# Expert rows returned to their tokens: token numbers through a table in device memory, a later request for half of the rows, and no padding matmuls in the last pair

## The chip, the cores and the metric

The kernel runs on one core of a Trainium2 chip. The metric is the device time of one execution in microseconds, lower is better; the number compared is the median over several runs. Everything is float32.

## What is computed

One layer of a hybrid backbone over 256 latent tokens of width 1024 (with 256 context tokens): a token mixer (neighbourhood attention, a gated scan and grouped-query attention, merged by gates), and then a mixture of experts. The change lies in the second part:

```python
def hierarchical_moe(h, w_gr, b_gr, w_er, b_er, w_gate, w_up, w_down):
    ...
    e_val, e_idx = lax.top_k(e_in, TOP_K)              # TOP_K = 2 of 16 experts
    w_sel = jax.nn.softmax(e_val, axis=-1) * p_group
    ...
    for e in range(N_EXPERTS):
        he = jax.nn.silu(h @ w_gate[e]) * (h @ w_up[e])
        y = y + combine[:, e:e + 1] * (he @ w_down[e])
    return y
```

After it the kernel adds `mod[5] * y` to the stream and applies a final RMS norm. Each token goes to a first and a second choice of expert.

## The kernel before

The expert part works on eight pairs of experts (pairs 0 to 7; LAST is 7). An expert has 64 slots for tokens (CAP), so a pair fills 128 slots. For each pair TensorE does, in this order: `gate` (16 matmuls with 512 columns, shown as 32 records, since every float32 matmul has two records), `up` (the same), the gathering of the first half of the next pair's tokens with a 0/1 selection matrix S (L1116), the turning of the hidden values (`turn_hidden`, L1186), the second half of that gathering, and `down` in two column halves (8 matmuls each, 16 records). `gate`, `up` and `down` are all recorded at L1163, in `two_experts`.

**Weights.** Each pair needs six halves of weights (gate 0, gate 1, up 0, up 1, down 0, down 1), numbered through as q = 0 to 47; a half is two loads of 1 MB, one for each expert (L387). They go through a ring of 11 places, and SyncE issues load after load on its queue, each as soon as its place is free. The last pair uses q = 42 to 47: up takes 44 and 45, down takes 46 and 47. TensorE waits for both loads of a half ahead of its first matmul (`take_half`).

**Rows of pairs 0 to 6.** VectorE scales a pair's result into `y_sb` (`experts_out`, L1722), and GpSimd writes its 128 rows with one indirect DMA (L565) to rows of the device array `y_rows`, which has one block of 256 rows for the first choices and one for the second. The row numbers stand in `token_rows`, one column for each pair. To make such a column, TensorE multiplies S with the token numbers (`tokens_of_slots`, L1126, 2 columns), and VectorE turns the sum into integers (`rows_of_tokens`, L1712). Rows out of bounds are skipped. Before `experts_out` writes `y_sb` again it waits for the write of the pair before.

**The return.** When the write of pair 6 has landed, GpSimd asks for `y_rows` in four reads of 512 KB (L570): two of first choices, two of second choices. VectorE multiplies each with the token's weight and adds it to `acc` (`gathered_back`, L1731).

**The last pair** stays on the chip: `scatter` multiplies the turned selection matrix with `y_sb` (L1210), one column half at a time, and VectorE adds the sums to `acc` (`scattered`, L1704). TensorE's order at the end is down 0, scatter 0, down 1, scatter 1. VectorE's order is: three reads gathered, `experts_out` of half 0, the fourth read gathered, `scattered` 0, `scaled_tokens` (L1697, the final gain on the first half of the columns), `experts_out` of half 1, `scattered` 1. After that only the final norm and the output are left.

**Padding.** In the last pair TensorE also runs matmuls whose result nobody reads (`stay_warm`, L1151): one ahead of each half of up, and two ahead of down 0.

All engines run their own instructions in order. Pairs over 64 tokens for an expert would go through later passes, which these inputs don't need.

Of the kernel before, what the change touches and what calls it, by code (L numbers as in the profile page):

```python
# [13 lines left out]
P = 128  # L14
D = 1024
KD = D // P
L = 256
# [124 lines left out]
def build(nc, d):  # L142

    ctx = ExitStack()
    with ctx:
# [121 lines left out]
        slot_of, slot_ok = keep(32, NT, NE), keep(4)  # L267
        slot_at, slot_w = keep(4), keep(4)
# [14 lines left out]
        token_of = keep(NT * NE, NT, NE)  # L283
# [42 lines left out]
        token_of_ready, token_sum, token_rows_ready = sem("token_of_ready"), sem("token_sum"), sem("token_rows_ready")  # L326
# [170 lines left out]
        def _(pool):  # L497
# [62 lines left out]

            pool.wait_ge(rows_cleared, 16 * 2 * NT)
            for n in range(LAST):
                pool.wait_ge(token_rows_ready, 2 * n + 2)
                pool.wait_ge(y_out, 2 * n + 2)
                pool.indirect_dma_start(d["y_rows"][:, :], bass.IndirectOffsetOnAxis(token_rows[:, n:n + 1], 0), y_sb, None,  # L565
                                        bounds_check=2 * L - 1, oob_is_err=False).then_inc(y_stored, 16)
            pool.wait_ge(up_ready, LAST)
            pool.wait_ge(y_stored, 16 * LAST)
            for q in range(2 * NT):
                pool.dma_start(y_back[:, q, :], d["y_rows"][q * P:q * P + P, :]).then_inc(y_in[q], 16)  # L570
# [177 lines left out]
        def _(pe):  # L748
# [371 lines left out]
            def tokens_of_slots(n, S):  # L1120

                pe.wait_ge(token_of_ready, 1)
                if n:
                    pe.wait_ge(token_rows_ready, 2 * n)
                for t in range(NT):
                    ins = pe.matmul(banks[7][:, 384 + 2 * n:386 + 2 * n], S[:, t, :], token_of[:, t, 2 * n:2 * n + 2],  # L1126
                                    start=(t == 0), stop=(t == NT - 1))
                ins.then_inc(token_sum, 1)

# [18 lines left out]
            def stay_warm(n):  # L1148

                for _ in range(n):  # L1150
                    pe.matmul(banks[1][:, :], ident, small[:, 0:512], start=True, stop=True)  # L1151

            def two_experts(bank, weights_at, parts, lhsT, q=None, n=None):

                for k in range(parts):
                    if q is not None and k % 4 == 0:
                        if q == 6 * LAST + 2:
                            stay_warm(1)
# [55 lines left out]
            for n in range(PAIRS):  # L1214
                gate(n, ring(6 * n), 6 * n)
                up(n, ring(6 * n + 2), 6 * n + 2)
                if n < LAST:
                    tokens_of_slots(n, S_now[n % 2])
                if n < LAST:
# [6 lines left out]
                for i in range(2):  # L1226
                    if n == LAST and i == 0:
                        stay_warm(2)
# [24 lines left out]
        def _(dve):  # L1253
# [11 lines left out]

            dve.memset(zeros, 0.0)
# [343 lines left out]
            def choices():  # L1610

                for j, oh in enumerate((oh1, oh2)):
                    link(dve.tensor_tensor(r_et, oh, slot_of, ALU.mult))
# [6 lines left out]
                dve.scalar_tensor_tensor(out=token_of, in0=oh2, scalar=float(L),  # L1620
                                         in1=sm("token").unsqueeze(2).broadcast_to([P, NT, NE]), op0=ALU.mult, op1=ALU.add)\
                   .then_inc(token_of_ready, 1)
# [84 lines left out]
            def rows_of_tokens(n):  # L1707

                dve.wait_ge(token_sum, n + 1)
                for e in range(2):  # L1710
                    part = slice(e * CAP, (e + 1) * CAP)
                    dve.tensor_scalar(token_rows[part, n:n + 1], banks[7][part, 384 + 2 * n + e:385 + 2 * n + e], 1024.0, None,  # L1712
                                      ALU.add).then_inc(token_rows_ready, 1)

# [24 lines left out]
            link(dve.tensor_tensor(slot_of, posm, sm("first_slot").unsqueeze(1).broadcast_to([P, NT, NE]), ALU.add))  # L1739
# [10 lines left out]
            for n in range(1, LAST + 1):  # L1750
# [3 lines left out]
                rows_of_tokens(n - 1)  # L1754
# [205 lines left out]
```

## Time and profile before

| | |
|---|---|
| median of 3 runs | 724.5 us (723.94 to 724.51) |
| the profiled execution's own time | 724.15 us |
| its span, first to last instruction | 722.4 us |
| busy: TensorE / VectorE / ScalarE / GpSimd | 701.3 / 296.9 / 112.2 / 172.6 us |
| expert pairs begin (first gathering) | 501.3 us |
| steady time of one pair | 25.4 us |
| last expert weights land, last row read lands | 702.2, 706.0 us |
| last matmul ends, last addition to `acc` ends | 715.7, 716.4 us |

Times of rows are microseconds from the first instruction. Matmuls are pipelined and their ends are modelled, so a row's end can stand up to some 0.1 us after the next row's start. What VectorE does is read best from its own timeline, and when a transfer was issued and landed from the views of its line.

### The profile page before, as it was taken

Reading aid. Unit: us, or ns where it says so; the run is one execution under the profiler, and the core shown is the slowest. Engines: PE = TensorE matmul, PEld = TensorE weight load, DVE = VectorE, ACT = ScalarE, POOL = GpSimd, SP = SyncE. Lnnn points to the kernel's source line nnn. Section 1 sums busy time; section 2 is a strip of 40 time slices with the busy share of each in tenths; the row PEclk is TensorE's granted clock in tenths of the full one; section 3 lists DMA queues with packets and bytes.
Section 4 is the critical chain, followed back from the end, with each engine's and each line's share of the span. In section 5 each row is a group of like instructions: output and inputs, shape, how many; then the busy total and the mean of one; then the engine's idle time right before and its main releaser. Section 6 shows DMA issues by size and latency. Waiting matters only on the chain.

```text
span 722.4 us, 7996 instructions
## 1 busy us (share of the span) xinstructions
PE 701.3 (97%) x3282; PEld 416.7 (58%) x3282; DVE 296.9 (41%) x507; ACT 112.2 (16%) x197; POOL 172.6 (24%) x126
## 2 busy tenths in 40 slices
PE   9999999999999999998999999999999999999995
PEld 5444586555775467776777788647434434443431
DVE  3439492778310475644343223325413212211315
ACT  4021011111000422221122230013000000000012
POOL 0008989789179000800000000000000000000010
PEclk9999999999999999999999999998999999999998
DMA  8994526762442332433481235995899999999991
GB/s 355 421 377 193 200 108 235 290 220 68 175 140 94 116 117 73 161 116 117 183 342 60 71 122 200 421 401 212 336 416 423 420 423 421 422 420 423 420 396 66
DMA packets 28933, 183.70 MB, mean 254 GB/s; under 512 B 3479, under 2 KB 5911, under 8 KB 13536
## 3 DMA queue, kind: packets, MB, share of 16 engines
q1 hardware_dynamic: 26880, 178.45, 62.4%
q0 software_dynamic: 1584, 3.97, 1.4%
q10 hardware_dynamic: 432, 0.75, 0.3%
q8 instruction: 27, 0.44, 0.2%
q14 instruction: 10, 0.08, 0.0%
HBM read 178.14 MB, written 6.82 MB: 256 GB/s over the span
## 4 chain that ended last, share of the span: by engine, by line
PE 91%; DMA 3%; DVE 2%; issue 2%; ACT 1%; SPq 0%; ACTq 0%; DVEq 0%; POOLq 0%
PE bank L1163 21%; PE bank L773 18%; PE bank L777 10%; PE bank L769 8%; PE bank L790 6%; PE bank L1116 4%; PE bank L995 4%; PE bank L796 4%; PE bank L920 2%; PE bank L941 2%; PE bank L822 2%; PE bank L928 2%; PE bank L783 2%; DMA y_rows<-sb,token_rows 1%; DMA sb<-y_rows 1%
## 5 line engine op out<-in xcount | busy, mean ns | idle before, releaser
L1163 PE MATMUL bank<-sb 128*64 128x512 f32 x768 | 167.5, 594 | 0.0
L773 PE MATMUL bank<-sb 128*128 128x256 f32 x576 | 128.5, 382 | 0.6 <-PE bank L769 0.3
L773 PEld LDWEIGHTS bank<-sb 128*128 128x128 f32 x576 | 108.1, 190 | 17.8 <-issue 3.8
L1163 PEld LDWEIGHTS bank<-sb 128*64 128x64 f32 x768 | 54.2, 137 | 106.7 <-issue 105.7
L565 POOL DMA_INDIRECT y_rows<-sb,token_rows x7 | 7.0, 997 | 371.5 <-DVE sb L1722 371.5
L525 POOL TENSOR_TENSOR sb<-sb 128x1024 f32<-128x1024 f32 x32 | 68.1, 2129 | 59.3 <-DMA sb<-ada_w 38.0
L1354 DVE COPY sb<-bank 128x512 f32<-128x512 f32 x45 | 29.2, 685 | 103.6 <-PE bank L928 66.2
L777 PE MATMUL bank<-sb 128*128 128x512 f32 x160 | 70.2, 593 | 0.3 <-PE bank L773 0.3
L769 PE MATMUL bank<-sb 128*128 128x512 f32 x128 | 55.8, 593 | 0.3 <-PE bank L995 0.3
L777 PEld LDWEIGHTS bank<-sb 128*128 128x128 f32 x160 | 29.9, 190 | 35.3 <-issue 35.3
L1687 DVE TENSOR_TENSOR sb<-sb,bank 128x512 f32<-128x512 f32 x8 | 5.5, 687 | 99.5 <-PE bank L1163 99.5
L790 PE MATMUL bank<-sb 128*128 128x256 f32 x192 | 42.2, 380 | 0.6 <-PE bank L790 0.6
L769 PEld LDWEIGHTS bank<-sb 128*128 128x128 f32 x128 | 23.9, 190 | 29.3 <-issue 29.3
L790 PEld LDWEIGHTS bank<-sb 128*128 128x128 f32 x192 | 36.2, 190 | 6.3 <-issue 1.5
L529 POOL TENSOR_TENSOR sb<-sb 128x512 f32<-128x512 f32 x24 | 35.7, 1488 | 1.9
L1116 PE MATMUL bank<-sb 128*128 128x128 f32 x256 | 31.7, 278 | 0.3 <-issue 0.3
L530 POOL TENSOR_TENSOR sb<-sb 128x512 f32<-128x512 f32 x24 | 30.6, 1273 | 1.9
L1116 PEld LDWEIGHTS bank<-sb 128*128 128x128 f32 x256 | 29.8, 192 | 0.4 <-issue 0.4
L995 PE MATMUL bank<-sb 128*128 128x512 f32 x64 | 29.0, 599 | 0.7 <-DVE sb L1306 0.7
L1678 DVE TENSOR_SCALAR sb<-bank,sb 128x128 f32<-128x128 f32 x64 | 21.9, 405 | 19.0 <-PE bank L1116 19.0
L661 ACT ACTIVATE sb<-bank,sb 128x512 f32<-128x512 f32 x32 | 21.8, 685 | 40.9 <-DVE sb L1469 40.8
L796 PE MATMUL bank<-sb 128*128 128x512 f32 x64 | 27.8, 592 | 0.0
(246 smaller groups left out, 684.2 us busy)
## 6 DMA issues: line engine op xcount, KB each, us to landing
sb<-expert_w SPq DMA_DIRECT2D x94, 1024.0 KB, 19.3
sb<-front_w SPq DMA_DIRECT2D x19, 2048.0 KB, 8.1
sb<-ada_w SPq DMA_DIRECT2D x32, 512.0 KB, 3.5
sb<-ada_mix SPq DMA_DIRECT2D x4, 2048.0 KB, 20.4
sb<-xcT SPq DMA_DIRECT2D x4, 512.0 KB, 6.2
sb<-front_w SPq DMA_DIRECT2D x4, 512.0 KB, 21.1
y_rows<-sb SPq DMA_DIRECT2D x4, 512.0 KB, 23.2
sb<-expert_w SPq DMA_DIRECT2D x4, 512.0 KB, 5.6
```

The costliest lines, as they stand in the source:

```text
L525: link(pool.tensor_tensor(w, w, cvec[:, k0:k0 + PART_K, 0:1].broadcast_to([P, PART_K, 512]), ALU.mult))
L529: link(pool.tensor_tensor(w[:, 0, :], w[:, 0, :], w[:, 1, :], ALU.add))
L530: ins = pool.tensor_tensor(ada_sum[g], ada_sum[g], w[:, 0, :], ALU.add)
L769: ins = pe.matmul(ps[:, :], lhs(w, k, i * P), hT[:, k, :], start=(k == 0), stop=(k == KD - 1))
L773: ins = pe.matmul(ps[:, c * L:(c + 1) * L], lhs(w, k, (2 * i + c) * P), hT[:, k, 0:L], start=(k == 0), stop=(k == KD - 1))
L777: ins = pe.matmul(ps[:, :], hT[:, k, i * P:(i + 1) * P], w[:, k * 512:(k + 1) * 512], start=(k == 0), stop=(k == KD - 1))
L790: ins = pe.matmul(ps[:, c * L:(c + 1) * L], lhs(w, k, (2 * i + c) * P, D), src[:, k, :], start=(k == 0), stop=(k == 3))
L796: ins = pe.matmul(ps[:, :], yT[:, k, i * P:(i + 1) * P], w[:, k * 512:(k + 1) * 512], start=(k == 0), stop=(k == KD - 1))
L995: ins = pe.matmul(banks[BANK_OF[i]][:, :], lhs(slot[0], k, i * P), hT[:, k, :], start=(k == 0), stop=(k == KD - 1))
L1116: ins = pe.matmul(banks[i][:, c * P:(c + 1) * P], x_nat[:, t, (4 * i + c) * P:(4 * i + c + 1) * P], S[:, t, :], start=(t == 0), stop=(t == ...
L1163: ins = pe.matmul(bank[e * CAP:(e + 1) * CAP, :], lhsT[:, k, e * CAP:(e + 1) * CAP], weights_at(k, e), start=(k == 0), stop=(k == parts - 1))
L1354: dve.tensor_copy(dst, shared_wait(n)[:, :]).then_inc(shared_out, 1)
```

## The change

- GpSimd gets a table in device memory, `slot_tokens`, with one number for each slot of pairs 0 to 6 (896 integers). It is first filled with 1024 (out of bounds) from a VectorE memset, at a quiet time. When the choices are known, VectorE works out for every token and choice its row in the table (`table_rows`) and the number to write there (`token_ids`). GpSimd writes them with four indirect DMAs of 128 numbers, waits for them, and reads the table back into `token_rows` with one DMA. After that all seven columns of row numbers are there.
- `tokens_of_slots` (TensorE) and `rows_of_tokens` (VectorE) go, for all seven pairs. `token_of` goes, two small VectorE instructions for `token_ids` and two for `table_rows` come.
- The two reads of second choices are issued only after weight half q = 46 (down 0 of the last pair) has landed. The two of first choices are issued as before.
- All `stay_warm` matmuls go.
- VectorE's order at the end becomes: `experts_out` half 0, four reads gathered, `scattered` 0, `experts_out` half 1, `scaled_tokens`, `scattered` 1.

```diff
+            table = d["slot_tokens"].rearrange("(p n) o -> p (n o)", n=LAST)
+            pool.wait_ge(rows_unused, 1)
+            pool.dma_start(table, token_rows[:, :]).then_inc(table_cleared, 16)
+            pool.wait_ge(ids_ready, 2)
+            pool.wait_ge(table_rows_ready, 1)
+            pool.wait_ge(table_cleared, 16)
+            for q in range(2 * NT):
+                pool.indirect_dma_start(d["slot_tokens"][:, :], bass.IndirectOffsetOnAxis(table_rows[:, q:q + 1], 0),
+                                        token_ids[:, q:q + 1], None, bounds_check=STORED - 1, oob_is_err=False)\
+                    .then_inc(table_filled, 16)
+            pool.wait_ge(table_filled, 16 * 2 * NT)
+            pool.dma_start(token_rows[:, :], table).then_inc(token_rows_in, 16)
+            pool.wait_ge(token_rows_in, 16)
             pool.wait_ge(rows_cleared, 16 * 2 * NT)
             for n in range(LAST):
-                pool.wait_ge(token_rows_ready, 2 * n + 2)
                 pool.wait_ge(y_out, 2 * n + 2)
                 pool.indirect_dma_start(d["y_rows"][:, :], bass.IndirectOffsetOnAxis(token_rows[:, n:n + 1], 0), y_sb, None,
                                         bounds_check=2 * L - 1, oob_is_err=False).then_inc(y_stored, 16)
             pool.wait_ge(up_ready, LAST)
             pool.wait_ge(y_stored, 16 * LAST)
             for q in range(2 * NT):
+                if q == NT:
+                    pool.wait_ge(w_in_[RING[(HALVES - 2) % len(RING)]], landed(HALVES - 2))
                 pool.dma_start(y_back[:, q, :], d["y_rows"][q * P:q * P + P, :]).then_inc(y_in[q], 16)
...
-            def tokens_of_slots(n, S):
-
-                pe.wait_ge(token_of_ready, 1)
-                if n:
-                    pe.wait_ge(token_rows_ready, 2 * n)
-                for t in range(NT):
-                    ins = pe.matmul(banks[7][:, 384 + 2 * n:386 + 2 * n], S[:, t, :], token_of[:, t, 2 * n:2 * n + 2],
-                                    start=(t == 0), stop=(t == NT - 1))
-                ins.then_inc(token_sum, 1)
...
-            def stay_warm(n):
-
-                for _ in range(n):
-                    pe.matmul(banks[1][:, :], ident, small[:, 0:512], start=True, stop=True)
...
                     if q is not None and k % 4 == 0:
-                        if q == 6 * LAST + 2:
-                            stay_warm(1)
                         take_half(q + k // 4)
...
                 if n < LAST:
-                    tokens_of_slots(n, S_now[n % 2])
-                if n < LAST:
                     gather(n + 1, S_now[(n + 1) % 2], (0,))
...
                 for i in range(2):
-                    if n == LAST and i == 0:
-                        stay_warm(2)
                     down(n, i, ring(6 * n + 4 + i), 6 * n + 4 + i)
...
+            dve.memset(token_rows[:, :], 1024).then_inc(rows_unused, 1)
             dve.memset(zeros, 0.0)
...
-                dve.scalar_tensor_tensor(out=token_of, in0=oh2, scalar=float(L),
-                                         in1=sm("token").unsqueeze(2).broadcast_to([P, NT, NE]), op0=ALU.mult, op1=ALU.add)\
-                   .then_inc(token_of_ready, 1)
+                link(dve.scalar_tensor_tensor(out=table_at, in0=slot_ok, scalar=-4096.0, in1=slot_at, op0=ALU.mult, op1=ALU.add))
+                dve.tensor_scalar(table_rows[:, :], table_at, 4096.0, None, ALU.add).then_inc(table_rows_ready, 1)
+                for j in range(2):
+                    dve.tensor_scalar(token_ids[:, NT * j:NT * j + NT], sm("token"), float(L * j), None, ALU.add)\
+                       .then_inc(ids_ready, 1)
...
                 modulate(n)
-                rows_of_tokens(n - 1)
...
             gated(LAST)
             turned_out(LAST)
-            gathered_back(range(2 * NT - 1))
             experts_out(LAST, (0,))
-            gathered_back((2 * NT - 1,))
+            gathered_back(range(2 * NT))
             scattered(LAST, (0,))
+            experts_out(LAST, (1,))
             dve.wait_ge(glast_in, 16)
             dve.wait_ge(scat_out, NT)
             scaled_tokens()
-            experts_out(LAST, (1,))
             scattered(LAST, (1,))
```

## Rows read from the trace of the kernel before

**Rows 1.** The page: the chain that ended last, by engine.
```profile
PE 91%; DMA 3%; DVE 2%; issue 2%; ACT 1%; SPq 0%; ACTq 0%; DVEq 0%; POOLq 0%
```
**Rows 2.** Busy time by stretch: length, PE, PEld, DVE, ACT, POOL, granted clock, DMA share, GB/s.
```profile
660.00:680.00 20.00, 20.00 (x114) 9.57 (x112) 4.07 (x12) 1.19 (x2) 0.21 (x1) 1.00 1.02 422
...
703.00:704.00 1.00, 1.00 (x8) 0.30 (x6) 1.00 (x2) 0.19 (x1) 0.00 (x0) 1.00 0.59 242
```
**Rows 3.** The chain in pair 6 (start, us, what), line L1126 alone, VectorE's timeline in pair 6.
```profile
671.41 0.54 PE bank L1126 x4
...
L1126 PE MATMUL bank<-sb x28: 251/251/272, 518.9 to 671.7; 128*128 128x2 f32 x28
...
671.51 0.69 DVE L1687 TENSOR_TENSOR sb<-sb,bank 128x512 f32<-128x512 f32 x1 [13.10 <-PE bank L1163]
```
**Rows 4.** TensorE's timeline in the last pair: start, us, instructions, idle time before.
```profile
689.88 1.13 PE L1151 MATMUL bank<-sb 128*128 128x512 f32 x2
...
694.52 1.13 PE L1151 MATMUL bank<-sb 128*128 128x512 f32 x2
695.58 3.65 PE L1163 MATMUL bank<-sb 128*64 128x512 f32 x16
...
702.38 3.65 PE L1163 MATMUL bank<-sb 128*64 128x512 f32 x16
707.22 1.96 PE L1210 MATMUL bank<-sb 128*128 128x512 f32 x4 [1.18 <-DVE sb L1722]
...
713.71 1.95 PE L1210 MATMUL bank<-sb 128*128 128x512 f32 x4 [0.95 <-DVE sb L1722]
```
**Rows 5.** Single weight loads of L387: issue time and, below, us from issue to landing.
```profile
L387 SPq DMA_DIRECT2D sb<-expert_w x1: 2122/2122/2122, 663.0 to 663.0; - x1
DMA to landing us min/median/max: 28.2/28.2/28.2
L387 SPq DMA_DIRECT2D sb<-expert_w x1: 6286/6286/6286, 665.6 to 665.6; - x1
DMA to landing us min/median/max: 30.5/30.5/30.5
```
**Rows 6.** The chain's step over the last row write, and the four reads' landings.
```profile
684.65 9.46 DMA y_rows<-sb,token_rows
...
L570 POOL DMA_DIRECT2D sb<-y_rows x4: 550/558/569, 694.7 to 696.3; - x4
...
DMA to landing us min/median/max: 7.7/8.7/9.7
```
**Rows 7.** VectorE's timeline at the end.
```profile
706.38 0.69 DVE L1722 TENSOR_TENSOR sb<-bank,sb 128x512 f32<-128x512 f32 x1
707.16 1.28 DVE L1731 SCALAR_TENSOR_TENSOR sb<-sb 128x1024 f32<-128x1024 f32 x1
708.52 1.38 DVE L1704 TENSOR_TENSOR sb<-sb,bank 128x512 f32<-128x512 f32 x2
710.00 1.29 DVE L1697 TENSOR_TENSOR sb<-sb 128x512 f32<-128x512 f32 x2
712.87 0.69 DVE L1722 TENSOR_TENSOR sb<-bank,sb 128x512 f32<-128x512 f32 x1 [1.58 <-PE bank L1163]
...
715.70 0.69 DVE L1704 TENSOR_TENSOR sb<-sb,bank 128x512 f32<-128x512 f32 x1 [0.17 <-PE bank L1210]
```
**Rows 8.** ScalarE's timeline: the copy of the last pair's turned hidden values.
```profile
700.77 0.60 ACT L708 ACTIVATE sb<-bank 128x512 f32<-128x512 f32 x1 [10.18 <-PE bank L1186]
```
**Rows 9.** TensorE's timeline and, below, busy time by stretch (columns as above) around 492 us.
```profile
491.37 3.79 PE L1078 MATMUL bank<-sb 128*128 128x20 f32 x24
...
493.00:495.00 2.00, 2.00 (x12) 2.00 (x11) 0.00 (x0) 0.51 (x1) 0.00 (x0) 0.50 1.04 438
```
**Rows 10.** GpSimd's first row write and the VectorE instruction that waits for it (timelines).
```profile
532.36 1.18 POOL L565 DMA_INDIRECT y_rows<-sb,token_rows  x1 [225.15 <-DVE sb L1722]
...
552.73 0.69 DVE L1722 TENSOR_TENSOR sb<-bank,sb 128x512 f32<-128x512 f32 x1 [1.59 <-PE bank L1163]
```

More of the change, by code:

```diff
@@ L266, in build @@
         passes_f = keep(1)
-        slot_of, slot_ok = keep(32, NT, NE), keep(4)
-        slot_at, slot_w = keep(4), keep(4)
+        table_of, slot_ok = keep(32, NT, NE), keep(4)
+        slot_at, slot_w, table_at = keep(4), keep(4), keep(4)
         SW_now, ST_now = at(C0 + 6144, NT, P), at(C0 + 6144 + NT * P, NT, P)
@@ L282, in build @@
         token_rows = ctx.enter_context(nc.sbuf_tensor("token_rows", [P, LAST], I32))
-        token_of = keep(NT * NE, NT, NE)
+        token_ids = ctx.enter_context(nc.sbuf_tensor("token_ids", [P, 2 * NT], I32))
+        table_rows = ctx.enter_context(nc.sbuf_tensor("table_rows", [P, 2 * NT], I32))
         masks = ctx.enter_context(nc.sbuf_tensor("masks", [P, LEVELS - 1, P], I8))
@@ L325, in build @@
         choice_ready = sem("choice_ready")
-        token_of_ready, token_sum, token_rows_ready = sem("token_of_ready"), sem("token_sum"), sem("token_rows_ready")
+        rows_unused, ids_ready, table_rows_ready = sem("rows_unused"), sem("ids_ready"), sem("table_rows_ready")
+        table_cleared, table_filled, token_rows_in = sem("table_cleared"), sem("table_filled"), sem("token_rows_in")
         rows_cleared = sem("rows_cleared")
@@ L1612, in choices @@
                 for j, oh in enumerate((oh1, oh2)):
-                    link(dve.tensor_tensor(r_et, oh, slot_of, ALU.mult))
+                    link(dve.tensor_tensor(r_et, oh, table_of, ALU.mult))
                     link(dve.tensor_reduce(slot_at[:, NT * j:NT * j + NT], r_et, AX.X, ALU.add))
@@ L1705, in scattered @@
                         ins.then_inc(scat_out, 1)
[L1707 to L1713, printed above, removed]
             def experts_out(n, halves=range(2)):
@@ L1738, in _ @@
             count_passes()
-            link(dve.tensor_tensor(slot_of, posm, sm("first_slot").unsqueeze(1).broadcast_to([P, NT, NE]), ALU.add))
+            link(dve.scalar_tensor_tensor(out=table_of, in0=posm, scalar=float(LAST),
+                                          in1=sm("first_row").unsqueeze(1).broadcast_to([P, NT, NE]), op0=ALU.mult, op1=ALU.add))
             choices()
@@ L1808 @@
                       ("ones", P), ("upto", P), ("iota", CAP), ("limits", MAXPASS - 1),
-                      ("rank", NE), ("first_slot", NE), ("token", NT), ("g_ffn", KD), ("lb", 8), ("hg_g", 1),
+                      ("rank", NE), ("first_row", NE), ("token", NT), ("g_ffn", KD), ("lb", 8), ("hg_g", 1),
                       ("gqn", HD), ("gqn_swapped", HD), ("gkn", HD), ("gkn_swapped", HD),
@@ L1826, in shape_constants @@
     rank = np.arange(NE, 0, -1, dtype=f)
+    e = np.arange(NE)
+    first_row = np.where(e < 2 * LAST, e % 2 * CAP * LAST + e // 2 - LAST, 4096).astype(f)
     t = np.arange(L)
@@ L1839, in shape_constants @@
         "limits": np.tile(np.arange(1, MAXPASS, dtype=f) * CAP, (P, 1)),
-        "rank": np.tile(rank, (P, 1)), "first_slot": np.tile(np.arange(NE, dtype=f) * CAP - 1, (P, 1)), "token": (i[:, None] + P * np.arange(NT)[None, :] - 1024).astype(f), "cos": cos.astype(f), "sin": sin.astype(f),
+        "rank": np.tile(rank, (P, 1)), "first_row": np.tile(first_row, (P, 1)), "token": (i[:, None] + P * np.arange(NT)[None, :]).astype(f), "cos": cos.astype(f), "sin": sin.astype(f),
     }
@@ L1956 @@
     d["y_rows"] = nc.dram_tensor("y_rows", (2 * L, D), F32).ap()
+    d["slot_tokens"] = nc.dram_tensor("slot_tokens", (STORED, 1), I32).ap()
     build(nc, d)
```

## The prediction

> **What bounds the kernel now.** I read the chain of work that ended last first: TensorE holds 91% of it [rows 1], so what leaves TensorE's queue counts unless something else is late behind it. The second view is the busy time by stretch: from 520 us on TensorE is busy all the time and so are the 16 DMA engines, at 422 GB/s [rows 2]. Both are full, so the question is which one has slack. For that I set the landing of single weight loads against the timeline of TensorE. Counted back from the last load, the second load of half 45 is issued at 663.0 and lands at 691.2, and that of half 46 is issued at 665.6 and lands at 696.1 [rows 5]; TensorE uses them at 695.6 and 702.4 [rows 4]. So TensorE is the bound, but the weights are only 4.4 and 6.3 us ahead of it, and an earlier release of places doesn't hasten them, since the engines are full. The last view is the end on VectorE. The four reads of rows are issued from 694.7 to 696.3 and land 7.7 to 9.7 us later, the last at 706.0 [rows 6]. The chain runs through the write of pair 6 and these reads to `gathered_back` and then to `experts_out` of half 0 at 706.38, just behind down 0, which ends at 706.03 [rows 4, 7]. Two paths are thus nearly tied there: both must get shorter, or nothing is gained.
>
> **Token numbers off TensorE.** L1126 has 28 records, four to a pair, and four take 0.54 us of the chain [rows 3]: 7 x 0.54 = 3.8 us, all ahead of gate of pair 7. The two VectorE instructions that go with each lie beside matmuls: nothing. The turning of the hidden values comes 0.54 us sooner behind up, but in pair 6 VectorE has `he` ready at 672.2 (671.51 + 0.69), and up ended at 671.4 with 1.9 us of gathering to come [rows 3], so it is still there.
>
> **The table.** It hangs on GpSimd, which waits for nothing else then. The choices are ready at about 510.5 us. Four indirect DMAs cost up to 1.2 us each by the row of the first row write, and 0.7 us between them: 518. Their landing and that of the read back aren't in this trace. From above I take the 9.5 us of the last row write, twice, from below 2.2 us, twice, the page's shortest landing (the pieces of the output). The column is then there between 523 and 538 us; the first row write is now at 532.4 [rows 10]. At worst it slips by 6 us. Behind it on GpSimd are only the other row writes, and the one who waits for it is `experts_out` of pair 1 at 552.7 [rows 10]: a write issued at 538 that takes 9 us has landed at 547. Cost zero; the cover ends when the write is issued later than about 543.5, and TensorE feels it only later still, when VectorE is late for pair 2's `he` at about 570. The clearing of the table and the extra memset lie in times in which their engines wait, and three more VectorE instructions of 0.2 us fall into its 7 us of idle time ahead of 519 us: zero.
>
> **Padding off TensorE.** One matmul ahead of each half of up moves the next by 1.06 us (694.52 to 695.58, and the same ahead of the first half), two ahead of down 0 end at 702.38 [rows 4]. But the copy of the turned hidden values ends at 701.4 [rows 8], so down 0 couldn't start before 701.5: there only 0.9 us is gained, and a gap takes the place of the rest. With the weights there in time the shift at down 0 would be 3.8 + 2.1 + 0.9 = 6.8 us.
>
> **What is late next: weight half 45.** Half 44 would be wanted at 689.9 - 3.8 = 686.1. Its second load lands two loads before the second one of half 45, and a load is 2.5 us at 422 GB/s, so at about 686: just in time. Half 45 would be wanted at 686.1 + 3.6 = 689.7 and lands at 691.2, so TensorE waits 1.5 us. Up ends at 691.2 + 3.6 = 694.8 instead of 699.2, down 0 starts 2.3 us later, as now from the end of up to the end of the copy, at 697.1 (half 46 landed at 696.1), and ends at 700.7. The shift is 5.3 us, not 6.8. `experts_out` of half 0 is done at 701.5 (0.1 + 0.69), scatter 0 runs from 701.65 to 703.55, and down 1 ends at 707.15; its half 47 had landed at 702.2, and the DMA share falls only in the slice from 703 us [rows 2].
>
> **The reads.** The write of pair 6 lands 3.8 us sooner, at 690.3 instead of 694.1 [rows 6]. The two reads of first choices are issued at 690.9 and 691.5 and land at about 698.6 and 699.8, ahead of `experts_out` of half 0. Those of second choices wait for half 46. They are the last instructions of GpSimd, so nothing is queued behind this wait, and VectorE alone waits for them. Landed at 696.1, with the 0.55 us from landing to issue that shows now, they are issued at 696.65 and 697.2. With 7.7 and 8.3 us [rows 6] they land at 704.4 and 705.5. The four 512 KB reads share the engines with the last weights; the first two now meet half 46, and may hold it up by some tenths: I take 705.7 for the last. For the duration the bounds are 5.6 us (the page's median for 512 KB pieces of weights) and 9.7 us. The order of requests moves, the bytes don't: the engines still have to carry the last weights and 2.1 MB of rows. The Trainium skill ("DMA: Bandwidth & Descriptors", section on the anatomy of a DMA on the gpsimd path) gives such a DMA about 2.0 us and its bytes at 436 GB/s, 3.2 us for 512 KB. This trace has 7.7 to 9.7 us with four reads and the weights in flight, and speaks against it. By the rule the last read would land by 701 us, and VectorE would be bound by its own work: 0.4 us less in the sum.
>
> **VectorE's end.** From 701.5 it gathers two reads (1.29 each) to 704.1, the third on landing to 705.7, the fourth from 705.7 to 707.0. `scattered` 0 takes 1.38 to 708.45, `experts_out` of half 1 is done at 709.15 (down 1 had ended at 707.15), scatter 1 starts at 709.3 and its first token block is there at 710.4. `scaled_tokens` (1.29) now lies beside it and ends at 710.5. Two additions of 0.69 with what lies between them end at 712.15. Now the last one ends at 716.39 [rows 7]. What follows is unchanged. **Sum: 716.39 - 712.15 = 4.2 us.** The profiled execution took 724.15 us, so 719.9; the median of the runs stands 0.35 us above it: **720.2 us**.
>
> **Rival 1, no waiting for weights.** If half 45 lands with its present lead over what TensorE needs (for instance because the row write of pair 6 now falls elsewhere in its way), `experts_out` of half 0 is done at 699.9, VectorE never waits for a read, and its own chain ends at 710.2 or so: 6.1 us gained, 718.4. Against it: the row write moves to an earlier time, into the stretch that carries halves 44 and 45.
>
> **Rival 2, the second choices come late.** The first reads hold up half 46 by the time of their 1 MB (2.5 us), and the second reads take 9.7 us: the last lands at 709, VectorE ends at 715.4 at worst, 714.5 more likely: 722.5. For it: of the last load now the landing is 702.2 where its neighbours are about 2.5 us apart and it is 4.0 us behind, so reads do slow weights.
>
> **Rival 3, the clock: the other side.** The trace shows the granted clock at 0.50, 1.2 GHz, from 493 us, while TensorE was never idle but ran 20-column matmuls [rows 9], and it stays low for some 6.8 us, to 499.7. The change takes the padding out of such a place: between up and down 0 of the last pair there would be 2.3 us with six records of short transposes and gaps, where now the two padding matmuls fill 1.8 us. The Trainium skill ("TensorE: Matmul & The Clock Gate", part 1) says that the throttled clock is the default and activity releases it; by that rule the padding has a use and this part of the change is wrong. The rows show that light work can cost the clock, but also that the gaps of 1.18 and 0.95 us near the end don't [rows 4]: the granted clock stays at 1.00 up to 715 us. Price: the work from down 0 on is 3.6 + 1.95 + 3.6 + 1.95 = 11.1 us at 2.4 GHz [rows 4]. A fall at 697 us for 6.8 us adds 3.4 us to down 0, VectorE then gathers all four reads behind it, and the end comes at about 715.2: 723.3, still faster. If the clock stays low to the end, all of it doubles, and the last addition ends at about 721.9: 729.9 us, slower. It decides from about 5.7 us added: more than half of those 11.1 us at 1.2 GHz.
>
> **Rival 4, the table is late.** If its small DMAs took not 2 to 9.5 us each but over 30 us in all, pair 1's `experts_out` would wait, and beyond 25 us more TensorE too: 725 us or above. Nothing in the rows speaks for it. That rows land in wrong places would be no matter of time.
>
> **How the numbers follow.** Chances: the forecast 0.60 (719.2 to 721.8), rival 1 0.12, rival 2 0.14, rival 3 0.10 (half of it with the short fall), rival 4 and the unforeseen 0.04. The bounds of the reads give 719.8 to 721.6, a half 46 delayed by 2.5 us 723.5, rival 1 718.4; the range is 718.0 to 723.8. 0.2% is 1.45 us, about what a measurement of this kernel can tell from no change. Faster by more than that (below 723.05) are the forecast, rival 1 and most of rival 2: 0.85. Within it are the rest of rival 2 and the short fall: 0.08. Slower are the long fall and rival 4: 0.07.
>
> **What the profile after would show.** L1126, L1712 and L1151 are gone and a pair takes 24.9 us instead of 25.4; if not, something waits there. In the last pair a gap of about 1.5 us stands ahead of the second half of up, released by a weight load (rival 1: no gap), and one of about 0.9 us ahead of down 0. The first row write is at 538 us or before, and `experts_out` of pair 1 doesn't wait for it. The write of pair 6 is issued at 680.9; the last read lands at 705.7. `experts_out` of half 1 starts behind `scattered` 0, not behind down 1: VectorE, held by the reads, is the bound at the end. The granted clock is 1.00 up to the last matmul. The prediction is wrong if the clock falls before it, if the reads of second choices land beyond 709, or if TensorE waits for weights already in pair 6, where I reckon with a lead of over 5 us.

## The result: slower, with the weights late and TensorE waiting

| | before | changed |
|---|---|---|
| median | 724.5 us (6 runs, 723.94 to 725.38) | 728.06 us (6 runs, 726.35 to 728.74) |
| ratio to before | | 1.0042 (95% interval 1.003 to 1.0054) |
| profiled execution, its span | 724.15, 722.4 us | 726.35, 723.9 us |
| down 0 of the last pair starts | 702.4 us | 703.6 us |
| last addition to `acc` ends | 716.4 us | 717.95 us |

The prediction said 720.2 us, 718.0 to 723.8, with 0.85 for faster. It was wrong in sign. The profiled execution is the fastest of the six, so the profile shows the least of the loss; the ratio counts all of them.

The steady part is as predicted: L1126, L1712 and L1151 of before are gone and a pair takes 24.96 us. But in the last pair TensorE's timeline shows what [rows 4] doesn't, four waits for weights (columns as there; `two_experts` is L1162 now, scatter L1209):

```profile
673.36 10.79 PE L1162 MATMUL bank<-sb 128*64 128x512 f32 x48
685.43 3.66 PE L1162 MATMUL bank<-sb 128*64 128x512 f32 x16 [1.27 <-DMA sb<-expert_w]
691.10 5.35 PE L1162 MATMUL bank<-sb 128*64 128x512 f32 x16 [2.01 <-DMA sb<-expert_w]
696.80 3.65 PE L1162 MATMUL bank<-sb 128*64 128x512 f32 x16 [0.35 <-DMA sb<-expert_w]
...
703.60 3.65 PE L1162 MATMUL bank<-sb 128*64 128x512 f32 x16 [1.64 <-DMA sb<-expert_w]
708.20 1.96 PE L1209 MATMUL bank<-sb 128*128 128x512 f32 x4 [0.94 <-DVE sb L1712]
710.09 3.65 PE L1162 MATMUL bank<-sb 128*64 128x512 f32 x16
715.27 1.96 PE L1209 MATMUL bank<-sb 128*128 128x512 f32 x4 [1.53 <-DVE sb L1712]
```

Down of pair 6 still starts 2.6 us sooner than before (673.36 instead of 676.0). Then the second half of gate waits for half 43, the two halves of up wait for 44 and 45, and by 696.80 TensorE is 1.2 us behind before. The first half of up takes 5.35 us for what takes 3.65. That is no second wait for weights: TensorE is busy all the time, and the granted clock is 0.50, so it runs at 1.2 GHz there, behind the idle gap of 2.01 us (columns as in [rows 2]):

```profile
691.50:694.50 3.00, 3.00 (x10) 1.15 (x8) 0.00 (x0) 0.00 (x0) 0.05 (x1) 0.50 1.00 415
```

This cost nothing at the end, because half 45 landed only at 696.7: at full clock TensorE would have waited longer for it. The last wait for weights is for half 46: down 0 could have begun at about 702.6, behind the copy of the turned values, and begins at 703.60. The chain that ended last says the same; it has one load of half 46 in it where before it had the row write and the reads [rows 6]:

```profile
670.39 33.07 DMA sb<-expert_w
703.47 0.14 issue
703.60 3.67 PE bank L1162 x16
```

The single load, issue and landing time as in [rows 5]: half 46 lands 33.1 us after 670.4, at 703.5. Before it was 696.1. Half 45 (667.7 + 29.0) lands at 696.7 instead of 691.2.

```profile
L389 SPq DMA_DIRECT2D sb<-expert_w x1: 6280/6280/6280, 670.4 to 670.4; - x1
DMA to landing us min/median/max: 33.1/33.1/33.1
```

The engines weren't idle. The place where the stream fell behind is found by going through the busy time by stretch of both kernels from left to right. First the changed kernel, then before, both columns as in [rows 2]; the last number is GB/s:

```profile
512.00:516.00 4.00, 4.00 (x20) 1.29 (x18) 0.75 (x2) 0.60 (x1) 3.09 (x4) 1.00 1.04 383
516.00:520.00 4.00, 4.00 (x23) 1.66 (x20) 0.51 (x1) 0.00 (x0) 0.37 (x1) 1.00 1.02 271
520.00:524.00 4.00, 4.00 (x36) 3.60 (x36) 2.03 (x7) 0.60 (x1) 0.00 (x0) 1.00 0.96 182
510.00:530.00 20.00, 20.00 (x112) 9.26 (x110) 6.98 (x23) 1.19 (x2) 4.56 (x5) 1.00 1.00 313
```

```profile
516.00:520.00 4.00, 4.00 (x23) 1.82 (x20) 0.69 (x1) 0.00 (x0) 0.00 (x0) 1.00 1.01 426
520.00:524.00 4.00, 4.00 (x35) 3.62 (x35) 1.71 (x6) 0.60 (x1) 0.00 (x0) 1.00 1.01 426
510.00:530.00 20.00, 20.00 (x112) 9.47 (x110) 6.76 (x21) 1.19 (x2) 0.00 (x0) 1.00 1.01 412
```

The DMA share is the same 1.0, but from 510 to 530 us the engines move 313 instead of 412 GB/s: 20 us x 99 GB/s = 2.0 MB less, which is 4.8 us of the stream. The busy share alone hides it. At that time GpSimd writes the table, four indirect DMAs of 128 four-byte numbers each, at most 2 KB in all (a number whose row is out of bounds, as for tokens of the last pair, is skipped):

```profile
511.48 1.04 POOL L570 DMA_INDIRECT slot_tokens<-token_ids,table_rows  x1 [203.28 <-DVE token_ids L1619]
...
524.83 0.58 POOL L574 DMA_DIRECT2D token_rows<-slot_tokens  x1 [8.46 <-DMA slot_tokens<-token_ids,table_rows]
532.09 0.99 POOL L579 DMA_INDIRECT y_rows<-sb,token_rows  x1 [6.68 <-DVE sb L1712]
```

GpSimd itself isn't late: the first row write is at 532.09 (532.36 in [rows 10]) and waits for VectorE, not for the table.

At the end VectorE is no longer held by the reads. It does all four in one go behind down 0 (compare [rows 7]):

```profile
707.36 0.69 DVE L1712 TENSOR_TENSOR sb<-bank,sb 128x512 f32<-128x512 f32 x1 [5.78 <-PE bank L1162]
707.97 5.19 DVE L1721 SCALAR_TENSOR_TENSOR sb<-sb 128x1024 f32<-128x1024 f32 x4
```

**Theory T** from here on: the table's small writes hold up the weight stream by 4.8 us, and the rest of the change is sound. **Rival R**: the table is harmless, and the earlier reads, the gate and the new order at the end are at fault.

### The profile page after: what moved, and what is told of

Same layout as the page of the kernel before. It is cut to its first block, busy times and chain, and to the rows that moved or that the text cites. A ratio compares the mean times of both kernels' runs of the same rounds, so it can differ in the third digit from the quotient of the medians.

```text
span 723.9 us, 7913 instructions
## 1 busy us (share of the span) xinstructions
PE 697.2 (96%) x3246; PEld 413.1 (57%) x3246; DVE 292.8 (40%) x497; ACT 112.2 (15%) x197; POOL 177.4 (25%) x132
## 4 chain that ended last, share of the span: by engine, by line
PE 80%; SPq 9%; DMA 6%; DVE 3%; issue 1%; ACT 1%; ACTq 0%; DVEq 0%
PE bank L789 18%; PE bank L1162 12%; PE bank L793 10%; SPq L389 9%; PE bank L785 8%; PE bank L806 6%; DMA sb<-expert_w 5%; PE bank L1011 4%; PE bank L812 4%; PE bank L1132 3%; PE bank L936 2%; PE bank L957 2%; PE bank L838 2%; PE bank L944 2%; PE bank L799 2%
## 5 line engine op out<-in xcount | busy, mean ns | idle before, releaser
L1162 PE MATMUL bank<-sb 128*64 128x512 f32 x768 | 169.8, 599 | 5.3 <-DMA sb<-expert_w 5.3
L1162 PEld LDWEIGHTS bank<-sb 128*64 128x64 f32 x768 | 55.0, 138 | 113.3 <-issue 106.2
L527 POOL TENSOR_TENSOR sb<-sb 128x1024 f32<-128x1024 f32 x32 | 66.6, 2081 | 59.9 <-DMA sb<-ada_w 36.0
L793 PE MATMUL bank<-sb 128*128 128x512 f32 x160 | 70.2, 593 | 0.3 <-PE bank L789 0.3
L785 PE MATMUL bank<-sb 128*128 128x512 f32 x128 | 55.8, 593 | 0.3 <-PE bank L1011 0.3
L570 POOL DMA_INDIRECT slot_tokens<-token_ids,table_rows x4 | 4.0, 994 | 204.2 <-DVE token_ids L1619 203.3
L1132 PE MATMUL bank<-sb 128*128 128x128 f32 x256 | 31.8, 278 | 0.3 <-issue 0.3
L1011 PE MATMUL bank<-sb 128*128 128x512 f32 x64 | 29.0, 599 | 0.7 <-DVE sb L1302 0.7
```

Of the source, the lines that this page charges most:

```text
L527: link(pool.tensor_tensor(w, w, cvec[:, k0:k0 + PART_K, 0:1].broadcast_to([P, PART_K, 512]), ALU.mult))
L785: ins = pe.matmul(ps[:, :], lhs(w, k, i * P), hT[:, k, :], start=(k == 0), stop=(k == KD - 1))
L793: ins = pe.matmul(ps[:, :], hT[:, k, i * P:(i + 1) * P], w[:, k * 512:(k + 1) * 512], start=(k == 0), stop=(k == KD - 1))
L1011: ins = pe.matmul(banks[BANK_OF[i]][:, :], lhs(slot[0], k, i * P), hT[:, k, :], start=(k == 0), stop=(k == KD - 1))
L1132: ins = pe.matmul(banks[i][:, c * P:(c + 1) * P], x_nat[:, t, (4 * i + c) * P:(4 * i + c + 1) * P], S[:, t, :], start=(t == 0), stop=(t == ...
L1162: ins = pe.matmul(bank[e * CAP:(e + 1) * CAP, :], lhsT[:, k, e * CAP:(e + 1) * CAP], weights_at(k, e), start=(k == 0), stop=(k == parts - 1))
```

## Experiments

The kernels were measured in four sessions, with the kernel before measured again beside them in each; the last column is its median there. These medians differ by 1.4 us, and its executions in the later three sessions spread from 723.4 to 730.3 us. Kernels of different sessions are therefore better compared by their ratios than by their medians.

| kernel | median us | ratio (95%) | before us |
|---|---|---|---|
| changed | 728.06 | 1.0042 (1.003 to 1.0054) | 724.5 |
| tail_only | 721.34 | 0.9937 (0.9916 to 0.9957) | 725.47 |
| table_only | 727.5 | 1.003 (1.0012 to 1.0047) | 725.47 |
| table_twice | 732.5 | 1.0081 (1.0048 to 1.0114) | 725.47 |
| dead4 | 726.72 | 0.9996 (0.9971 to 1.0022) | 725.86 |
| dead512 | 722.88 | 0.9958 (0.9938 to 0.9977) | 725.86 |
| dead4_spread | 721.77 | 0.9941 (0.9921 to 0.9961) | 725.86 |
| table_spread | 721.57 | 0.9954 (0.9931 to 0.9976) | 724.88 |
| tail_old_order | 727.24 | 1.0017 (0.9993 to 1.0042) | 724.88 |
| tail_ungated | 721.38 | 0.994 (0.992 to 0.996) | 724.88 |
| gather | 726.2 | 1.0018 (0.9999 to 1.0037) | 725.47 |
| gather_used | 720.58 | 0.9934 (0.9909 to 0.9959) | 725.86 |
| gather_used_pad | 719.92 | 0.9912 (0.988 to 0.9943) | 724.88 |

### The two halves of the change, apart

**tail_only** is the kernel before with the three edits that don't concern the table (padding, gate on the second choices, VectorE's order):

```diff
-                        if q == 6 * LAST + 2:
-                            stay_warm(1)
...
-                    if n == LAST and i == 0:
-                        stay_warm(2)
...
+                if q == NT:
+                    pool.wait_ge(w_in_[RING[(HALVES - 2) % len(RING)]], landed(HALVES - 2))
...
-            gathered_back(range(2 * NT - 1))
             experts_out(LAST, (0,))
-            gathered_back((2 * NT - 1,))
+            gathered_back(range(2 * NT))
             scattered(LAST, (0,))
+            experts_out(LAST, (1,))
...
             scaled_tokens()
-            experts_out(LAST, (1,))
```

> Tail parts alone: the kernel before without padding matmuls, with the new VectorE order and the gated second reads, token numbers still by TensorE. Theory T (the table's 4-byte writes hold up the weight stream by about 4.8 us): the weights land as before, so up ends at 697.1, down 0 at 703.0, the last addition at about 714.0: 2.4 us faster than before, about 722. Rival R (the new requests and order at the end are at fault, the table is harmless): at least 2 us slower than before, 727.

**table_only** is the changed kernel with those three edits taken back.

> Table alone: token numbers through the table, but padding, VectorE order and ungated reads as before. Theory T: the weight stream is 2 MB (4.8 us) behind from 530 us on, TensorE waits in the last pair in spite of being 3.8 us earlier: slower than before, 727 to 729. Rival R: TensorE saves 3.8 us and the reads come as much earlier: 720.7.

Measured: 721.34 and 727.5 us. R is dead: the end of the change alone gains 0.6%, and the table alone loses 0.3% in spite of the matmuls it takes from TensorE. The two don't add up: together they lose 0.42%. While down 0 waits for half 46, a shorter way to it is worth nothing. In tail_only no wait for weights shows in the last pair; down 0 starts at 698.99 behind the copy:

```profile
675.98 20.83 PE L1158 MATMUL bank<-sb 128*64 128x512 f32 x96
...
698.99 3.65 PE L1158 MATMUL bank<-sb 128*64 128x512 f32 x16 [0.69 <-ACT sb L710]
```

### Is it the small writes, and what about them?

**table_twice** is the changed kernel with the four writes repeated into a spare array ahead of the read back:

```diff
+            for q in range(2 * NT):
+                pool.indirect_dma_start(d["spare_table"][:, :], bass.IndirectOffsetOnAxis(table_rows[:, q:q + 1], 0),
+                                        token_ids[:, q:q + 1], None, bounds_check=STORED - 1, oob_is_err=False)\
+                    .then_inc(table_filled, 16)
```

> The changed kernel with its four small writes issued a second time, into a spare array. Theory T: the stream loses its 2 MB a second time and every later half lands 4.8 us later: 732 to 733, 4 to 5 us above the changed kernel. Rival R: four more small DMAs beside the matmuls cost nothing at the end: 728.

Measured: 732.5 us, 4.4 us above the changed kernel by the medians, about as T had it (7.0 above before in its session, where the changed kernel was 3.6 above before in its own: 3.5 by that). From 510 to 540 us the busy time by stretch has 284 GB/s (before: 411): 3.8 MB lost, nearly twice the 2.0, and half 46 lands at 708.6 (675.6 + 33.0), 5.1 us later than in the changed kernel. In the traced execution, 6.3 us above the changed kernel's, down 0 also ran at granted clock 0.50 and took 5.32 us for 3.65, so 1.7 us of that are the clock's.

**dead4** adds the writes to tail_only with nobody reading them, and the two VectorE instructions that make their row numbers; TensorE's work stays as in tail_only:

```diff
+            for q in range(2 * NT):
+                pool.indirect_dma_start(d["dead"][:, :], bass.IndirectOffsetOnAxis(table_rows[:, q:q + 1], 0),
+                                        ident[:, q:q + 1], None, bounds_check=STORED - 1, oob_is_err=False)\
+                    .then_inc(table_filled, 16)
+            pool.wait_ge(table_filled, 16 * 2 * NT)
```

> tail_only (721.3 us) plus four indirect writes of 128 numbers of 4 bytes, to the rows of the table, which nobody reads; token numbers still by TensorE. Theory T (these writes alone hold the stream up, whoever uses them): about 2 MB fewer weights between 510 and 530 us, halves 42 to 47 land 4.8 us later, 726 to 728. Rival (the read back, or TensorE's earlier pace, is what made weights late): 721 to 722.

**dead512** writes `ident[:, :]`, 512 bytes a piece, and **dead4_spread** writes 4 bytes again, but to row numbers times 128.

> As dead4, but each of the 128 pieces of a write has 512 bytes instead of 4 (256 KB in all). If the small size of a piece is the cause: only the bytes cost, 0.6 us of the stream, and 721 to 722. If the number of pieces or of indirect DMAs is the cause: as dead4, 726 to 728.

> As dead4, 4-byte pieces again, but each 512 bytes or more from the next in device memory. If pieces that share a block of memory wait for each other: much less than dead4, 721 to 723. If a 4-byte piece is slow by itself: as dead4, 726 to 728.

Measured: 726.72, 722.88 and 721.77 us, against 721.34 without any of them. Three stretches of dead4, and the same three of dead4_spread:

```profile
516.00:520.00 4.00, 4.00 (x25) 1.76 (x21) 0.69 (x1) 0.00 (x0) 0.29 (x1) 1.00 1.36 406
520.00:524.00 4.00, 4.00 (x36) 3.73 (x36) 1.60 (x5) 0.60 (x1) 0.00 (x0) 1.00 0.71 64
510.00:530.00 20.00, 20.00 (x114) 9.50 (x112) 7.11 (x23) 1.20 (x2) 4.13 (x4) 1.00 1.01 330
```

```profile
516.00:520.00 4.00, 4.00 (x25) 2.04 (x22) 0.69 (x1) 0.00 (x0) 0.00 (x0) 1.00 1.02 422
520.00:524.00 4.00, 4.00 (x35) 3.55 (x35) 1.93 (x6) 0.60 (x1) 0.00 (x0) 1.00 1.02 430
510.00:530.00 20.00, 20.00 (x114) 9.61 (x112) 6.82 (x21) 1.20 (x2) 4.12 (x4) 1.00 1.01 409
```

So at most 512 writes of 4 bytes into an array of 3.5 KB bring 422 to 430 GB/s down to 64 for 4 us. The share of 1.36 in one slice and 0.71 in the next says that single slices are rough here; over the 20 us it is 330 instead of 412 GB/s in tail_only, 1.6 MB. The same number of the same writes cost nothing that can be seen when their targets lie 512 bytes or more apart. The number of pieces, their size alone and the indirect form are each ruled out, and so is the read back, which dead4 doesn't have. That writes into one block of device memory wait for each other is the likeliest reason; the runs show the dependence on the distance, not the mechanism. How far apart is enough was not tried.

dead512 lies 1.5 us above tail_only, where 0.6 was expected for its bytes. Its trace puts this ahead of the writes. The gathering for pair 0 (L1128 there, L1118 in tail_only) runs at granted clock 0.50 and takes 6.45 instead of 3.81 us, so gate of pair 0 begins 2.0 us later (506.96 instead of 505.00), and the first of the writes is issued only at 513.09. First dead512, with its busy time by stretch, then tail_only:

```profile
500.57 6.45 PE L1128 MATMUL bank<-sb 128*128 128x128 f32 x32
501.00:506.00 5.00, 5.00 (x25) 5.00 (x25) 1.94 (x8) 0.00 (x0) 0.00 (x0) 0.50 0.00 0
```

```profile
501.26 3.81 PE L1118 MATMUL bank<-sb 128*128 128x128 f32 x32 [0.35 <-issue]
505.00 5.37 PE L1158 MATMUL bank<-sb 128*64 128x512 f32 x24
```

It helps to count from the start of that gate to the end of the last addition to `acc`: 208.35 us in tail_only, 208.35 in dead512, 208.36 in dead4_spread and 210.78 in dead4. In the traced executions only the dense writes cost anything.

The executions vary: dead4 ran from 723.08 to 728.87 us, dead4_spread from 721.44 to 723.19. The four of dead4 up to 724.16 have a mean granted clock of 0.995 to 0.997, the six from 726.68 on one of 0.990 to 0.994. The traced one (724.09) is of the first kind, so how much of the median's 5.4 us above tail_only is the stream and how much the clock is not shown. In the traced one it is 2.4 us, and TensorE waits for weights for 3.0 us there.

**table_spread** is the test on the change itself, with only the distance changed:

```diff
-            table = d["slot_tokens"].rearrange("(p n) o -> p (n o)", n=LAST)
+            table = d["slot_tokens"].rearrange("(p n w) o -> p n (w o)", n=LAST, w=P)[:, :, 0:1]
...
-                dve.tensor_scalar(table_rows[:, :], table_at, 4096.0, None, ALU.add).then_inc(table_rows_ready, 1)
+                dve.tensor_scalar(table_rows[:, :], table_at, 4096.0, float(P), ALU.add, ALU.mult).then_inc(table_rows_ready, 1)
```

> The changed kernel whole, only its table's numbers stand 512 bytes apart (row number times 128). Theory S (4-byte writes close together in device memory hold up the stream; the rest of the change is sound): the stream is on time, the last addition ends at about 712, 719.5 to 721, clearly faster than before. Rival: the read back, now 896 pieces of 4 bytes, holds the stream up in its turn: 723 or above.

Measured: 721.57 us, faster than before by 0.46%. The median lies 0.6 us above the expected end, its runs spread from 720.44 to 725.38, and 13 GB/s are still missing over the 20 us against before (0.26 MB, 0.6 us), with 368 GB/s in the slice in which the table is read back in 896 pieces:

```profile
524.00:528.00 4.00, 4.00 (x20) 1.29 (x18) 1.73 (x5) 0.00 (x0) 0.00 (x0) 1.00 1.02 368
...
510.00:530.00 20.00, 20.00 (x112) 9.22 (x110) 6.84 (x22) 1.19 (x2) 5.00 (x5) 1.00 1.01 399
```

The changed kernel's last addition ends 5.0 us later than this one's (717.95 and 712.97), where the difference in lost bytes is worth 4.2 us. By the ratios the two kernels lie 6.4 us apart; what the rest is stays open.

The run also splits the delay of the last halves. Its half 46 is issued at 666.2 and lands 31.8 us later, at 698.0:

```profile
L389 SPq DMA_DIRECT2D sb<-expert_w x1: 6303/6303/6303, 666.2 to 666.2; - x1
DMA to landing us min/median/max: 31.8/31.8/31.8
```

696.1 before, 698.0 here, 703.5 in the changed kernel: 5.5 us come with the dense table. Of the other 1.9 us, 0.6 are the missing 0.26 MB. The row write and the first reads are asked for some 3 and 4.5 us sooner than before, but they don't show as the reason for the rest: gather_used, below, asks for them as early (680.91 and 690.37) and has half 46 at 695.5. It carries some 0.2 MB less in its software queue than before; what the difference is stays open.

### The parts of the end

**tail_old_order** is tail_only with VectorE's old order, **tail_ungated** is tail_only with all reads asked for at once.

> tail_only (721.3 us) with VectorE's old order at the end (three reads gathered ahead of experts_out of half 0), padding still gone, reads still gated. If the two paths are tied as the prediction said: down 0 is done sooner, but experts_out of half 0 comes only after the reads, at about 706: 724 to 725, no gain over before. Rival (dropping the padding is the whole gain, the order doesn't matter): 721 to 722.

> tail_only (721.3 us) with all four reads asked for at once, as before. There the wait for half 46 held the reads of second choices back for only 0.4 us, so: 721 to 722, no difference. Rival (the gate protects the last weights, down 0 or down 1 waits without it): 723 or above.

Measured: 727.24 and 721.38 us. The gate is worth nothing here (its wait was 0.4 us). Without the new order the end gains nothing, and I had expected less of a loss: without padding and in the old order the kernel isn't at 724 to 725 but at 727.24. TensorE's timeline and the stretches with the granted clock show why:

```profile
699.22 3.65 PE L1158 MATMUL bank<-sb 128*64 128x512 f32 x16 [0.69 <-ACT sb L710]
707.80 3.75 PE L1205 MATMUL bank<-sb 128*128 128x512 f32 x4 [4.92 <-DVE sb L1715]
711.48 3.79 PE L1158 MATMUL bank<-sb 128*64 128x512 f32 x16
```

```profile
704.00:708.00 4.00, 0.20 (x1) 0.23 (x2) 3.69 (x5) 0.00 (x0) 0.00 (x0) 0.62 0.14 56
708.00:710.00 2.00, 2.00 (x3) 0.94 (x4) 1.15 (x2) 0.00 (x0) 0.00 (x0) 0.50 0.00 0
```

Down 0 is done sooner, but `experts_out` still stands behind three reads, TensorE is idle for 4.92 us, the granted clock falls to 0.50 (1.2 GHz), and scatter 0 takes 3.75 instead of 1.95 us. This is the clock of the prediction's rival 3, though at another place, which the changed order closes. It agrees with the Trainium skill ("TensorE: Matmul & The Clock Gate", part 1), by which the throttled clock is the default and activity releases it. The new order with the padding kept was not run, so what the order is worth by itself isn't known.

### A way without token numbers

**gather** drops the table and the matmuls alike: `y_sb` is stored in slot order, and the reads pick the rows by token.

```diff
-                pool.indirect_dma_start(d["y_rows"][:, :], bass.IndirectOffsetOnAxis(token_rows[:, n:n + 1], 0), y_sb, None,
-                                        bounds_check=2 * L - 1, oob_is_err=False).then_inc(y_stored, 16)
+                pool.dma_start(d["y_rows"][n * P:n * P + P, :], y_sb).then_inc(y_stored, 16)
...
-                pool.dma_start(y_back[:, q, :], d["y_rows"][q * P:q * P + P, :]).then_inc(y_in[q], 16)
+                pool.indirect_dma_start(y_back[:, q, :], None, d["y_rows"][:, :], bass.IndirectOffsetOnAxis(row_of[:, q:q + 1], 0),
+                                        bounds_check=STORED - 1, oob_is_err=False).then_inc(y_in[q], 16)
```

> No table and no token numbers at all: y_sb is stored in slot order by plain DMAs, and the four returned reads become indirect reads with one row number for each token and choice (nothing is cleared first). No padding, new VectorE order, reads not gated. Theory T: nothing stalls the stream, TensorE is 3.8 us earlier: about 720, as the prediction's sum had it. Rival R (early reads hold up the last weights): 724 or above.

Measured: 726.2 us, a miss. I had overlooked that a plain store carries empty slots too, where the indirect one skips them. Its software queue, and that of the next kernel:

```profile
q0 software_dynamic: 1584, 5.54, 1.9%
```

```profile
q0 software_dynamic: 1584, 3.75, 1.3%
```

TensorE waits 2.59 us for weights ahead of 689.93, before the first read is issued at 690.34, so that wait isn't the reads' doing. It waits again ahead of down 0, and there the clock falls as well (TensorE's timeline and a stretch):

```profile
702.12 5.08 PE L1139 MATMUL bank<-sb 128*64 128x512 f32 x16 [2.17 <-DMA sb<-expert_w]
702.00:705.00 3.00, 2.88 (x8) 1.14 (x10) 0.00 (x0) 0.40 (x2) 0.00 (x0) 0.50 1.02 419
```

Down 0 takes 5.08 instead of 3.65 us: 1.4 us of the miss are the clock, at the very place where rival 3 had it.

**gather_used** stores only used slots, with row numbers from the experts' counts (six small VectorE instructions beside gate of pair 0), and gates the second choices:

```diff
-                pool.dma_start(d["y_rows"][n * P:n * P + P, :], y_sb).then_inc(y_stored, 16)
+                pool.indirect_dma_start(d["y_rows"][:, :], bass.IndirectOffsetOnAxis(store_rows[:, n:n + 1], 0), y_sb, None,
+                                        bounds_check=STORED - 1, oob_is_err=False).then_inc(y_stored, 16)
```

> No table, no token numbers; rows are stored at their slot's place, but only the used slots (row numbers from the experts' counts, empty ones out of bounds), so the stores carry 1.8 MB as before and not the 3.7 MB of the run gather; the returned reads are indirect, those of second choices wait for half 46; no padding, new VectorE order. Theory T plus: what made gather slow was its 1.9 MB more of stores, 4.4 us of the stream; here they are gone: 719 to 720, at or below tail_only. Rival (indirect reads are slow in themselves): 724 or above.

Measured: 720.58 us. The 1.8 MB are gone and with them 5.6 us by the medians (the bytes are worth 4.3 us; the two kernels also differ in gather's half clock in down 0, in the gate, worth nothing in tail_ungated, and in the early clearing). But its last scatter ran at half clock, behind an idle gap of 2.23 us:

```profile
708.53 3.09 PE L1199 MATMUL bank<-sb 128*128 128x512 f32 x4 [2.23 <-DVE sb L1710]
```

```profile
708.50:712.00 3.50, 3.09 (x4) 0.82 (x4) 2.11 (x4) 1.36 (x5) 0.00 (x0) 0.60 0.02 5
```

**gather_used_pad** fills that gap:

```diff
                     if n == LAST:
+                        if i == 1:
+                            for _ in range(2):
+                                pe.matmul(banks[3][:, :], ident, small[:, 0:512], start=True, stop=True)
                         scatter(n, (i,))
```

> gather_used (720.6 us; the granted clock fell to 0.50 after an idle gap of 2.2 us ahead of the last scatter, which then took 3.1 instead of 1.95 us) with two matmuls whose result nobody reads between down 1 and scatter 1. If that clock loss is real and the gap its place: last scatter at full clock, 1 us less, 719.5. Rival (the fall comes by chance, or elsewhere): 720.5, and the padding may cost up to 0.3 us.

```profile
708.24 1.98 PE L1218 MATMUL bank<-sb 128*128 128x512 f32 x4
710.89 1.96 PE L1199 MATMUL bank<-sb 128*128 128x512 f32 x4 [0.67 <-DVE sb L1713]
```

Measured: 719.92 us, the lowest median of all, 0.9% below before. The scatter is back at 1.96 us. The gain over gather_used is 0.7 of the expected 1 us, and the two intervals overlap, so that the padding pays is shown by the trace and not by the times. The traced execution is the slowest of its six: its gathering for pair 0 took 6.61 us at granted clock 0.50, as in dead512. From the start of pair 0's gate to the last addition it needs 206.84 us, gather_used 207.88.

## Why the prediction was wrong, point by point

- **The table, "cost zero": this is the step that failed.** I priced its DMAs as latency of GpSimd and asked who waits for their landing. That part held: the column was there at 530.7 (524.83 + 5.9), inside my 523 to 538. What I didn't price is what they do to the engines they share with a stream that I had just found full and only 4.4 us ahead of TensorE. The price was 2.0 MB, 4.8 us of the stream. Rival 4 had the right culprit at 0.04, but as a wait of `experts_out` in pair 1, which never came.
- **The landing times of [rows 5], taken as fixed: wrong.** I took them so because the engines are full ("the bytes don't" move). They hold only while nothing lowers what full engines carry.
- **Token numbers off TensorE: right as a mechanism, 3.8 us was too much.** A pair takes 24.96 instead of 25.40 us, so 0.44 and not 0.54 us are saved for each, 3.1 in all. It is lost again at halves 43 to 46.
- **Half 45 as the next limit: right as a mechanism.** In table_spread TensorE waits 1.39 us there, where the sum had 1.5; in gather_used 0.61.
- **Half 46 "held up by some tenths": open.** In table_spread it lands 1.9 us later than before, near the 2.5 us of rival 2, and TensorE is idle for 1.19 us ahead of down 0 instead of the 0.69 us that the copy takes in tail_only. But in gather_used, with the reads as early, it lands at 695.5, not later than before.
- **Padding and order, 0.9 us at down 0 and the rest: right.** In tail_only the last addition ends at 713.35 against 714.0 expected. In table_spread it ends at 712.97 and in gather_used at 712.34, where the prediction's sum had 712.15. Its sum was thus near that of a kernel whose table costs nothing. That it comes so near gather_used is partly luck: 1.1 us of the 712.34 are the scatter at half clock, which the sum doesn't have.
- **Rival 3, the clock: not the cause of the loss, but the fall came.** I had written that the clock would stay at 1.00 up to the last matmul. In the changed kernel it was 0.50 from 691.5 to 694.5 us, in up, where the wait for half 45 hid the loss; from 701 to 720 us it is 1.00 in every slice. In gather and table_twice it fell at the place that rival 3 named, ahead of down 0, and cost 1.4 and 1.7 us. Each time TensorE had first waited for weights.
- **The gate on second choices**: in the changed kernel it released the reads at 703.95, 7 us later than in the sum, because half 46 was late; even so VectorE didn't wait for them, since all moved together.
- **The chances don't add up to what is said of them.** By their parts "slower" is 0.05 + 0.04 = 0.09 and not 0.07. That changes nothing in the verdict.

## What to carry to other kernels

When the engines are full and a stream is only just ahead of its user, every DMA has two prices: its latency for whoever waits, and what it takes from the stream; the second is read from GB/s by stretch, not from the busy share, which stayed at 1.0 while a quarter of the bandwidth was gone. Scatter small numbers to targets well apart in device memory, or find a form that needs no numbers (reading by index what was stored in order), and let empty rows be skipped. Padding matmuls and the order of work on the engine that TensorE waits for belong together: dropped without the new order the padding left 727.2 us, with it 721.3. Late weights open gaps as well, and in three of the traced kernels without padding the clock fell behind one; in table_only, which has the padding and waits for the same weights, it stayed at 1.00.

## What the hardware showed that I had not expected

- At most 512 four-byte writes into 3.5 KB of device memory take 1.6 to 2.0 MB from a stream of about 420 GB/s; in the worst 4 us of dead4 it ran at 64 GB/s. The same writes at 512 bytes or more apart: 422 to 430 GB/s. The Trainium skill ("DMA: Bandwidth & Descriptors", specifications) says that below 512 bytes an engine reads, modifies and writes. That covers both forms alike, and only the dense one was slow here: for pieces of 4 bytes it is the distance that decides in these runs.
- Executions of one kernel differ by more than the change is worth: 6 us between the fastest and the slowest run of dead4, with the lower mean clock in the slower ones.
- The granted clock fell to 0.50 behind idle gaps of 4.92 us (tail_old_order), 2.23 (gather_used), 2.17 (gather), 2.01 (the changed kernel) and 1.81 us (table_twice). It stayed at 1.00 behind gaps of 2.59 us (gather) and 2.01 and 1.88 us (table_twice), and behind those of 0.9 to 1.5 us near the end. So the length of one gap doesn't decide.
